# Expert stages: one scatter of whole rows, and the row buffer as three more landing slots

## The reference, cut to what matters

```
def expert_choice_ffn(h, router, w1, w3, w2):
    cap = max(1, EC_FACTOR * T // N_EXPERTS)
    aff = softmax(einsum('btd,de->bte', h, router), -1)
    gate, idx = lax.top_k(swapaxes(aff, 1, 2), cap)
    xs = h[idx]                                          # per expert: cap rows of 1024
    hid = silu(einsum('becd,edf->becf', xs, w1)) * einsum('becd,edf->becf', xs, w3)
    ys = einsum('becf,efd->becd', hid, w2) * gate[..., None]
    return zeros((T, D)).at[idx].add(ys)
...
x = x + g2 * expert_choice_ffn(h, moe_router[i], moe_w1[i], moe_w3[i], moe_w2[i])
```

## Time and profile before

| | |
|---|---|
| timed runs | 4167.84 us median of 3 (4167.56 to 4175.71) |
| span of the profiled execution, first to last instruction | 4167.8 us |
| busy over the span | PE 87%, DVE 47%, ACT 27%, POOL 16% |
| expert stage of layer 0 | about 576 to 1198 |
| expert stage of layer 1 | about 2124 to 2672 |
| weights of the two stages | 384 loads of 1 MB, median 18.1 us from issue to landing |
| scatters | 48 (32 in layer 0, 16 in layer 1), median 9.2 us to landing |
| gathers | 32, median 10.6 us to landing |

### The profile page before, as it was taken

One profiled execution on the slowest core, in us unless ns is written; L12 is line 12 of the kernel. 1 busy time (PEld: TensorE's weight loads), 2 busy tenths in 40 slices (PEclk: granted clock), 3 DMA queues, 4 the chain that ended last, 5 costly groups with the idle time before them and its releaser, 6 DMA issues. The chain is left out here.

```text
span 4167.8 us, 71056 instructions
## 1 busy us (share of the span) xinstructions
PE 3632.9 (87%) x29972; PEld 2565.1 (62%) x29972; DVE 1958.1 (47%) x3688; ACT 1143.7 (27%) x2375; POOL 648.3 (16%) x687
## 2 busy tenths in 40 slices
PE   5978878999979897989769777798899997899999
PEld 4845663444448783858553222396788776677877
DVE  4688751001045556756640000255477445656762
ACT  2124510000023413434310000225432223663221
POOL 0014400111102301525200000014100001430000
PEclk8998888999989998989889999999999998999999
DMA  4142248999941213010269999810123221012322
GB/s 171 58 162 63 77 185 315 394 395 394 394 146 80 89 49 115 4 43 4 95 233 401 402 401 400 309 56 21 63 91 96 91 93 43 22 47 66 96 91 81
DMA packets 195492, 660.04 MB, mean 158 GB/s; under 512 B 27708, under 2 KB 86076, under 8 KB 145368
## 3 DMA queue, kind: packets, MB, share of 16 engines
q1 hardware_dynamic: 182392, 621.16, 39.7%
q0 software_dynamic: 12784, 34.35, 3.2%
HBM read 626.01 MB, written 29.44 MB: 157 GB/s over the span
## 5 line engine op out<-in xcount | busy, mean ns | idle before, releaser
L3488 DVE TENSOR_TENSOR ffn_w_lo<-ffn_landing,ffn_w_hi 128x1024 fp32r<-128x1024 f32 x128 | 156.9, 1226 | 295.7 <-ACT ffn_w_hi L3466 295.7
L3437 PE MATMUL ffn_ps<-ffn_inT_hi,ffn_w_hi 128*128 128x512 f32 x704 | 279.2, 397 | 3.5 <-PEq L70 3.5
L3437 PE MATMUL ffn_ps<-ffn_inT_lo,ffn_w_hi 128*128 128x512 f32 x704 | 278.1, 395 | 0.0
L3437 PE MATMUL ffn_ps<-ffn_inT_hi,ffn_w_lo 128*128 128x512 f32 x704 | 277.4, 394 | 0.0
L2044 PE MATMUL up_ps<-w_quarter,rowsT 128*64 128x512 f32 x1024 | 235.9, 602 | 38.5 <-DMA w_quarter<-in_moe_w 38.4
L2044 PE MATMUL down_ps<-w_quarter,hiddenT 128*64 128x512 f32 x1024 | 236.4, 601 | 32.3 <-DMA w_quarter<-in_moe_w 30.3
L2044 PE MATMUL gate_ps<-w_quarter,rowsT 128*64 128x512 f32 x1024 | 236.6, 608 | 27.6 <-DMA w_quarter<-in_moe_w 18.8
L1960 POOL DMA_INDIRECT summed_dram<-gains_then_rows,part_row x48 | 74.7, 1557 | 932.1 <-DVE gains_then_rows L2174 927.2
L2104 ACT ACTIVATE rowsT<-misc_ps 128x384 f32<-128x384 f32 (+1 forms) x64 | 27.9, 438 | 603.9 <-PE misc_ps L2033 602.3
L2167 DVE TENSOR_TENSOR gain_then_hidden<-up_ps,gain_then_hidden 128x768 f32<-128x768 f32 (+1 forms) x32 | 26.4, 825 | 352.2 <-PE up_ps L2056 181.3
L2044 PEld LDWEIGHTS down_ps<-w_quarter,hiddenT 128*64 128x64 f32 x1024 | 68.6, 136 | 190.5 <-issue 129.9
(11 more groups left out here) (727 smaller groups left out, 8348.0 us busy)
## 6 DMA issues: line engine op xcount, KB each, us to landing
w_quarter<-in_moe_w SPq DMA_DIRECT2D x384, 1024.0 KB, 18.1
ffn_landing<-in_f_w_up SPq DMA_DIRECT2D x88, 512.0 KB, 3.5
ada_ring<-in_ada_w SPq DMA_DIRECT2D x80, 512.0 KB, 5.4
ffn_landing<-in_f_w_down SPq DMA_DIRECT2D x44, 512.0 KB, 3.5
w_landing<-in_od_w_in SPq DMA_DIRECT2D x13, 1024.0 KB, 6.1
w_landing<-in_a_w_in SPq DMA_DIRECT2D x12, 1024.0 KB, 5.0
ada_landing<-in_ada_w SPq DMA_DIRECT2D x8, 1024.0 KB, 12.5
w_landing<-in_ev_w_in SPq DMA_DIRECT2D x6, 1024.0 KB, 5.7
```

Source lines behind the costliest of these rows:

```text
L3437: mm = nc.tensor.matmul(ps[c % 4][:, :], w[:, c % NP, cols], h[:, k, :], start=(k + i == 0), stop=(k == KD - 1 and i == 2))
L3488: nc.vector.tensor_tensor(wl[:, c % NP, :], land[:, c % NL, :], wh[:, c % NP, :].bitcast(F32), ALU.subtract).then_inc(split, 1)
```

## The change

The scatter writes whole rows of 4 KB by the token list, one indirect DMA an expert: 96 rows in layer 0, 64 in layer 1. So that the rows lie whole, `rows_out` writes each part to the partitions of its rows, beside its neighbours: six VectorE instructions (2 of 64 x 512 and 4 of 32 x 256) instead of two in layer 0, two (64 x 512) instead of one in layer 1. The part lists `pidx` are no longer built: fewer small VectorE instructions, two fewer transposes and two fewer copies (layer 0; one and one in layer 1). And once the rows x are stored in `sum_dram`, their buffer (six tiles, 24 KB a partition) serves as three more slots of the ring: 19 slots instead of 16, of which quarters 16 to 18 are loaded as soon as the stores of x have landed.

```
-        rows, ys = [shared[0:R, c, :] for c in range(2)], [shared[:, 2 + c, 0:W] for c in range(2)]
+        rows, ys = ([shared[0:R, 2 * b + c, :] for c in range(2)] for b in range(2))
...
-        land += [st.sb(f"w_quarter{c}", [P, QK, D]) for c in range(n_free + n_turn, NL)]
+        land += [st.sb(f"w_quarter{c}", [P, QK, D]) for c in range(n_free + n_turn, NQ)]
+        land += [x[:, c:c + QK, :] for c in range(0, NT, QK)]
+        NL = len(land)
...
+        landed = list(landed) + [st.sem(f"row_tiles_landed{c}") for c in range(NL - NQ)]
...
             sp.wait_ge(h_stored, 16 * nt)
-            for g in range(n_free + n_turn, len(order)):
+            for g in range(n_free + n_turn, NQ):
                 load(g)
-            sp.wait_ge(y_added, 16 * NS * E)
+            sp.wait_ge(x_stored, 16 * nt)
+            for g in range(NQ, len(order)):
+                load(g)
+            sp.wait_ge(y_added, 16 * E)
...
-            def scatter(e, part, to, cols):
-                nc.gpsimd.indirect_dma_start(out=to,
-                                             out_offset=bass.IndirectOffsetOnAxis(ap=pidx[:, part, e:e + 1], axis=0),
-                                             in_=ys[e % 2][:, cols], in_offset=None, compute_op=ALU.add) \
-                    .then_inc(y_added, 16)
+            def scatter(e):
+                nc.gpsimd.indirect_dma_start(out=sum_dram,
+                                             out_offset=bass.IndirectOffsetOnAxis(ap=idx[:, e:e + 1], axis=0),
+                                             in_=ys[e % 2], in_offset=None, compute_op=ALU.add).then_inc(y_added, 16)
...
-                scatter(e, 0, lat_rows, slice(0, LW))
-                if CR:
-                    scatter(e, 1, ctx_rows, slice(LW, W))
+                scatter(e)
...
             for part in range(NS):
-                c = (1 + 2 * part) * E
-                nc.tensor.transpose(misc[1][:, c:c + E], parts_i[:, part, :], ident[0:E, 0:E])
-                mm = nc.tensor.transpose(misc[1][:, c + E:c + 2 * E], parts_v[:, part, :], ident[0:E, 0:E])
+                c = (1 + part) * E
+                mm = nc.tensor.transpose(misc[1][:, c:c + E], parts_v[:, part, :], ident[0:E, 0:E])
...
-                for part, cols in ((0, slice(0, LW)), (1, slice(LW, W)))[0:NS]:
-                    last = nc.vector.scalar_tensor_tensor(out=ys[e % 2][:, cols], in0=py[:, cols],
-                                                          scalar=gall[:, part, e:e + 1], in1=g2r[:, cols],
-                                                          op0=ALU.mult, op1=ALU.mult)
+                for part, n, r0, r, cols in ((0, 2, 0, LR, slice(0, LW)), (1, 4, LR, CR, slice(LW, W)))[0:NS]:
+                    for j in range(n):
+                        own, w = slice(j * r, (j + 1) * r), D // n
+                        last = nc.vector.scalar_tensor_tensor(out=ys[e % 2][r0:r0 + r, j * w:(j + 1) * w],
+                                                              in0=py[own, cols], scalar=gall[own, part, e:e + 1],
+                                                              in1=g2r[own, cols], op0=ALU.mult, op1=ALU.mult)
...
-                for j in range(n):
-                    last = nc.vector.tensor_scalar(parts_i[:, part, j * r:(j + 1) * r], topi[:, r0:r0 + r], float(n), float(j),
-                                                   ALU.mult, ALU.add)
```

More of the change, by code:

```diff
@@ L1843, in mixture @@
     G1, GE = 8, 12
-    NL = len(landed)
+    NQ = len(landed)
     n_turn = nt // 2
-    n_free = NL - 2 * n_turn
+    n_free = NQ - 2 * n_turn
     h_dram = nc.dram_tensor(f"normed_dram_{i}", (nt * P, D), F32).ap()
     sum_dram = nc.dram_tensor(f"summed_dram_{i}", (nt * P, D), F32).ap()
-    lat_rows = sum_dram.rearrange("t (n d) -> (t n) d", d=LW)
-    ctx_rows = sum_dram.rearrange("t (n d) -> (t n) d", d=CW)
     with Stage(nc) as st:
@@ L1869, in mixture @@
         topi = st.sb("top_token", [E, R])
-        parts_v, parts_i = (left[:, c * NS * P:(c + 1) * NS * P].rearrange("e (s r) -> e s r", s=NS) for c in range(2))
+        parts_v = left[:, 0:NS * P].rearrange("e (s r) -> e s r", s=NS)
         idx = st.sb("row_token", [R, E], mybir.dt.uint32)
-        pidx = st.sb("part_row", [P, NS, E], mybir.dt.uint32)
         gall = st.sb("part_gates", [P, NS, E])
@@ L1909, in mixture @@
         y_added = st.sem("rows_added")
+        landed = list(landed) + [st.sem(f"row_tiles_landed{c}") for c in range(NL - NQ)]
         block = st.block()
-        before = list(loaded)
+        before = list(loaded) + [0] * (NL - NQ)
         for g in range(len(order)):
-            loaded[g % NL] += 1
+            if g % NL < NQ:
+                loaded[g % NL] += 1
         def tile_rows(t, dram):
@@ L1975, in _ @@
                 if e:
-                    pool.wait_ge(y_added, 16 * NS * e)
-                scatter(e, 0, lat_rows, slice(0, LW))
-                if CR:
-                    scatter(e, 1, ctx_rows, slice(LW, W))
+                    pool.wait_ge(y_added, 16 * e)
+                scatter(e)
         @block.tensor
@@ L2171, in rows_out @@
                 if e >= 2:
-                    dve.wait_ge(y_added, 16 * NS * (e - 1))
-                for part, cols in ((0, slice(0, LW)), (1, slice(LW, W)))[0:NS]:
-                    last = nc.vector.scalar_tensor_tensor(out=ys[e % 2][:, cols], in0=py[:, cols],
-                                                          scalar=gall[:, part, e:e + 1], in1=g2r[:, cols],
-                                                          op0=ALU.mult, op1=ALU.mult)
+                    dve.wait_ge(y_added, 16 * (e - 1))
+                for part, n, r0, r, cols in ((0, 2, 0, LR, slice(0, LW)), (1, 4, LR, CR, slice(LW, W)))[0:NS]:
[4 more added lines that the diff above has]
+                                                              in1=g2r[own, cols], op0=ALU.mult, op1=ALU.mult)
                 last.then_inc(y_ready, 1)
@@ L2204, in _ @@
             for part, n, r0, r in ((0, 2, 0, LR), (1, 4, LR, CR))[0:NS]:
-                nc.vector.tensor_copy(parts_v[:, part, :].rearrange("e (n r) -> e n r", n=n),
-                                      topv[:, r0:r0 + r].unsqueeze(1).broadcast_to([E, n, r]))
-                for j in range(n):
-                    last = nc.vector.tensor_scalar(parts_i[:, part, j * r:(j + 1) * r], topi[:, r0:r0 + r], float(n), float(j),
-                                                   ALU.mult, ALU.add)
+                last = nc.vector.tensor_copy(parts_v[:, part, :].rearrange("e (n r) -> e n r", n=n),
+                                             topv[:, r0:r0 + r].unsqueeze(1).broadcast_to([E, n, r]))
             last.then_inc(top_ready, 1)
@@ L2213, in _ @@
             for part in range(NS):
-                c = (1 + 2 * part) * E
-                nc.vector.tensor_copy(pidx[:, part, :], misc[1][:, c:c + E])
-                last = nc.vector.tensor_copy(gall[:, part, :], misc[1][:, c + E:c + 2 * E])
+                c = (1 + part) * E
+                last = nc.vector.tensor_copy(gall[:, part, :], misc[1][:, c:c + E])
             last.then_inc(idx_ready, 1)
```

## The result

The changed kernel takes 4178.5 us (median of 20 runs, 4169.18 to 4185.51); the kernel before, on the same chip, 4167.53 us (20 runs, 4156.27 to 4183.31). The ratio is 1.0023, 95% interval 1.0016 to 1.0030: 9.6 us slower (6.7 to 12.5). The interval lies wholly above 1; against the 0.2% (8.3 us) that the prediction took as the limit of what can be told from no change, the ratio lies just above and the interval on both sides.

A forecast was written before the change was run, and what follows sets the result against it. TensorE was taken to bound layer 0, the DMA engines layer 1. Terms +3.3 (gather 0), +3.7 (end of layer 0), 0 (scatter), -0.8 (dry moment), +0.7 (end of layer 1) gave +6.9, 4174.7 us; range 4162 to 4183.

The forecast's parts named there:

- Gather 0: Start of layer 0: the first gather shares the engines with three early loads, so TensorE starts 3.3 us later (+2.1 to +6.5).
- TensorE has no slack after that, so all of it reaches the end: Layer 0 after gather 0: the whole +3.3 us of TensorE's later start carries through to the stage's end.
- The rival of the undelayed gather: Start of layer 0: early loads don't delay gather 0, layer 0 starts 0.9 us earlier, total 4170.5 us; chance 0.13.
- The shorter routing: Before the first gather: fewer VectorE instructions, transposes and copies issue it 0.9 us earlier in layer 0, about half in layer 1.
- End of layer 0: Expert 14's and 15's row pieces on VectorE delay the last scatter and the reload of x, +3.7 us.
- the last scatter then starts 3.66 us later: End of layer 0: VectorE's pieces, 2.97 us an expert or +1.83, delay it twice, by expert 14's and expert 15's rows.
- The scatter's price: Both layers' scatters: the same bytes in fewer, larger packets cost the same, since price goes by bytes; 0 us.
- the count case: Layer 1's scatters: rows cost by count, so it gains 9.5 us, period 32.0, total 4165.2 us; chance 0.10.
- the half partitions: Layer 1's scatters from 64 partitions: price per byte doubles, +18.5 us, period 33.9, total 4193 us; chance 0.10.
- The dry moment: Layer 1 around 2181: the load queue briefly runs dry, and the three more slots give back 0.8 us (0 to 2.2).
- the +0.7 of its last pieces: End of layer 1: two VectorE pieces take 1.42 us, +0.67, and the last expert's delay counts.

The follow-up runs named there:

- slots alone: The kernel before with only the three more ring slots added, scatters and pieces as before; ratio 1.0002 (0.9991 to 1.0013) to the kernel before.
- before with the new end: The kernel before with only the last down product moved to the gate's PSUM tile and expert 15's copies put ahead of expert 14's rows; ratio 0.9999.
- new end: The changed kernel with expert 15's copies ahead of expert 14's pieces and the last down product in the gate's PSUM tile; ratio 1.0001 to the kernel before.
- rows alone: The changed kernel without the three more slots (16 slots, whole-row scatters kept); ratio 1.0016 (1.0006 to 1.0027) to the kernel before.
- loads held: The changed kernel with the three early loads held until TensorE has turned gather 0's rows; ratio 1.0008 (0.9999 to 1.0017) to the kernel before.
- experiments with an idle wait: The kernel before with one or two idle VectorE product pairs ahead of expert 14's rows; TensorE's wait 2.58 or 3.89 us, last product 10.68 or 12.37 us.
- half wait: The kernel before with one idle VectorE product pair ahead of expert 14's rows; TensorE's wait 2.58 us, last product 10.68 us, no ratio.

## Why the prediction came out right, and where its terms did not

The forecast of +6.9 us lies just inside the ratio's interval, 2.7 us under its middle, and the main mechanisms were the ones named. At the end of layer 0, however, the cost of the clock was left out and the pieces were taken too short. In the pair of profiles the sum still comes near (8.0), since the clock gave back 1.5 us at the first end, which nobody had forecast either: that the two met is luck.

**Gather 0, forecast +3.3.** Right in place and size: counted from the first issue of the stage before, the gather goes out at 633.2 and TensorE starts at 642.8 (633.4 and 643.4 forecast). The gather behind the loads takes 9.0 to 9.5 us (10.0 forecast), and the first rows come 2.7 us later in the pair, 3.2 by the means of all kernels. At the turning of expert 15's hidden rows, however, only 1.04 of the pair's 2.7 are left. The clock makes the difference. Stretches of the kernel before, then of the one after:

```profile
640.00:647.00 7.00, 6.38 (x20) 2.74 (x22) 0.00 (x0) 2.27 (x3) 0.91 (x1) 0.50 0.19 57
647.00:648.00 1.00, 1.00 (x4) 0.24 (x2) 0.00 (x0) 0.00 (x0) 0.00 (x0) 0.56 0.00 0
648.00:652.00 4.00, 4.00 (x22) 1.14 (x18) 0.00 (x0) 0.00 (x0) 0.00 (x0) 1.00 0.00 0
```
```profile
641.00:645.00 4.00, 3.42 (x14) 1.73 (x15) 0.00 (x0) 2.26 (x3) 0.91 (x1) 0.50 0.99 305
645.00:646.00 1.00, 1.00 (x6) 0.26 (x4) 0.00 (x0) 0.00 (x0) 0.00 (x0) 0.73 0.89 274
646.00:652.00 6.00, 6.00 (x42) 2.02 (x42) 0.00 (x0) 0.00 (x0) 0.00 (x0) 1.00 0.12 25
```

TensorE starts on the half clock both times; before, it gets the full one 7 to 8 us after its first rows (640.04); after, some 5 us after them (640.73). The 64-row part of the first gate product takes 8.41 us for 9.91, 1.5 us given back. The delay alone does not bring the clock up sooner, as the same part shows in before, slots alone, and before with the new end, in that order:

```profile
642.15 9.91 PE L2044 MATMUL gate_ps<-w_quarter,rowsT 128*64 128x512 f32 x32 [0.58 <-ACT rowsT L2104]
```
```profile
645.60 9.81 PE L2051 MATMUL gate_ps<-w_quarter,rowsT 128*64 128x512 f32 x32 [0.58 <-ACT rowsT L2111]
```
```profile
642.76 9.01 PE L2044 MATMUL gate_ps<-w_quarter,rowsT 128*64 128x512 f32 x32 [0.58 <-ACT rowsT L2103]
```

Slots alone starts as late as the changed kernel and takes 9.81, the new end, as late too, 8.57; the four kernels whose first end has no edit take 9.01 to 9.94. What sets the moment stays open. With this part taken off, the way from the first rows to the turning of expert 15's hidden rows is 524.9 to 525.1 us in all ten kernels. So "TensorE has no slack after that, so all of it reaches the end" holds, and the pair's 1.04 owes 1.5 us to that moment of the clock. The rival of the undelayed gather is out: it would have had TensorE start earlier than before. With the 2.6 us of the means in place of the pair's 1.04, layer 0's loss is 10.0 us, and the ratio's interval holds that too.

**The shorter routing, forecast 0.9 us.** It is there at the issue (57.05 for 58.09), and no gain from it is to be seen behind that while quarters 10 to 15 are in the queue (rows alone, loads held). The forecast had it inside the +3.3, against a gather of 10.0 us that took 9.5, so the sum lost little by it.

**End of layer 0, forecast +3.7, measured +7.39.** The step that failed is the sum "the last scatter then starts 3.66 us later". Its way is right: the pieces delay TensorE once and the last scatter once more. Its sizes are not, and it takes TensorE's product as fixed. The pieces take 3.50 us, not 2.97, since they don't overlap as the pair did: the wait grows by 2.47 and the last pieces by 2.36, for 1.83 each. And the product takes 2.98 us more, since the longer wait was followed by the half clock; the experiments with an idle wait show that cause by itself, and the new end its removal. The size of this second term is not settled: in the three other kernels that waited as long the product took 1.5 to 1.7 us more, and the end of the two of them that have the pieces 5.9 and 6.2 us more.

On the pieces, the Trainium skill, "VectorE: DVE Perf Modes", section "Two Vector instructions with no wait between them", says that an instruction whose operands start in another group of 32 partitions than the last one's is held until the earlier have finished. By that rule the estimate is the sum of their lengths, 3.40 us, and the trace's 3.49 to 3.50 agree better with it than with the overlap I took.

**The scatter's price, forecast 0.** Right. Layer 1's period is 32.65, and 32.65 to 32.86 over all ten kernels; the count case wanted 32.0 and the half partitions 33.9. TensorE in layer 0 does not wait for weights in the steady state (busy for all of its 33.87 us). The queues in one microsecond of layer 1 with loads and a scatter, 2341 to 2342 (packets, MB, share), of the changed kernel, answering to the earlier trace rows:

```profile
q0 software_dynamic: 29, 0.12, 59.3%
q1 hardware_dynamic: 25, 0.18, 45.0%
```

A 4 KB packet holds an engine for 59.3% of 16 us / 29 = 0.33 us; a 2 KB packet held it for 40.3% of 48 us / 110 = 0.18. Against 0.413 MB in an undisturbed microsecond, 0.23 MB are missing for 0.12 scattered: 0.56 us, some 4.7 us per MB (to the two digits of the row), as before.

The half-partitions rival drew on the Trainium skill, "SBUF — State Buffer", section "Door 1: The DMA port swizzle (why `[64,N]` ≈ `[32,N]`)". The scatter from 64 partitions beside full loads doesn't show that halving in layer 1's period, and the measurement decides for this stage.

**The dry moment, forecast -0.8.** Right in the queue, not to be seen in the stage. The load queue of the changed kernel from 2186 to 2190, which is as far into the stage as the four microseconds of the earlier trace rows are before:

```profile
q1 hardware_dynamic: 139, 1.01, 77.2%
```

The queue moves 1.01 MB for 0.74 before; with the 1.4 us that gather 2 was priced at taken off, 1.07 would go, so it is as good as full. The load queue over the first 70 us of layer 1's stage, of before, rows alone, slots alone and after, in that order:

```profile
q1 hardware_dynamic: 5288, 25.96, 95.5%
```
```profile
q1 hardware_dynamic: 5282, 25.91, 94.0%
```
```profile
q1 hardware_dynamic: 5327, 26.28, 95.7%
```
```profile
q1 hardware_dynamic: 5328, 26.29, 95.7%
```

The two kernels with slots move 0.32 to 0.38 MB more, 0.8 to 0.9 us at 0.413 MB/us. Layer 1's stage, however, takes 546.18 and 546.57 us without them, 545.79 and 546.58 with them: the profiles' own spread covers the gain, and the +0.7 of its last pieces (1.51 for 0.75 measured) as well.

## What to carry to other kernels

At a stage's ends, follow an added delay on an off-path engine to TensorE and ask what its longer wait does to the granted clock: here 2.5 us of added waiting cost 1.5 to 3 us more in the product behind it. Putting the copies that TensorE needs ahead of the work that nobody awaits took both away. A deeper ring was free in the steady state here and cost 3 us where it was first filled; hold its first loads until the small transfer that the path awaits has landed.

## What was not expected of the hardware

At the end of layer 0's stage a wait of 3.75 to 3.89 us between full-clock products was followed by 1.2 GHz for part of the next 7 us in all four kernels that had one there, and a wait of 2.58 us or less in none of the six others. The length alone doesn't decide, though. In layer 1's stage TensorE has waits of 2.10 us in the kernel before and of 2.40 us in the changed one:

```profile
2425.64 3.16 PE L2044 MATMUL down_ps<-w_quarter,hiddenT 128*64 128x512 f32 x8 [2.10 <-DMA w_quarter<-in_moe_w]
```
```profile
2282.03 1.94 PE L2044 MATMUL up_ps<-w_quarter,rowsT 128*64 128x512 f32 x8 [2.40 <-DMA w_quarter<-in_moe_w]
```

Behind the first the granted clock is 0.60 in the mean of 3 us and eight matmuls take 3.16 us; behind the second it stays at 1.00 and eight take 1.94. So a wait of two microseconds can already cost the clock, and the half wait's 1.00 is no proof that it is safe.

And a 96-row gather of 4 KB rows, 4.2 to 5.8 us from its issue to the turned rows with the load queue nearly empty, takes 9.0 to 9.5 us behind three loads of 1 MB, and 7.5 to 8.2 us if it is issued one to three microseconds earlier, into the tail of the loads before.
